# Other SBUF places for the operands of TensorE's matmuls, and one chunk temporary moved to PSUM

## The chip, the cores and the metric

The kernel runs on one core of a Trainium2 chip (trn2). The metric is the device time of one execution in microseconds; the time before is 1974.9 us, the median of 3 runs (1974.86 to 1975.0).

## What is computed

One layer of a decoder trunk on 512 tokens with 2048 features, all in float32. It has two halves:

```
x = LN(alpha*x + mixer(x))                       # pooling, convolution, two sparse attentions
gate, up = split(x @ w_gate_up)                  # 2048 -> 2 x 5632
x = LN(alpha*x + (silu(gate)*up) @ w_down)       # 5632 -> 2048
```

The mixer begins with a projection `x @ w_in` and ends with `mix @ w_out`.

## The kernel before, in words

**Precision.** Most products are split into three passes: each operand is kept as a high part (`fp32r`) and a low part (what the high part leaves), and PE computes high x high, high x low and low x high into one PSUM bank. So every block of weights is loaded by DMA, rounded to its high part by ACT (or POOL) and subtracted by DVE (or POOL) for its low part, before PE may read it. In the trace each pass has a line of its own: L795 to L797 (projection and first gate/up chunks; weights stationary, activations moving), L1030 to L1032 (output projection; activations stationary, slabs moving), L1148, L1150 and L1152 (chunks), L1197, L1199 and L1201 (down units), L1237 to L1239 (tail).

**Stages.** Until about 480 us the projection and the attention run, until 662 us the output projection, until 710 us the first two of 44 chunks of 128 hidden features. Then comes a list of 62 units (`FF_UNITS`), 42 chunk units and 20 down units, in groups of six: three chunks, two downs, one chunk. A tail forms the last four chunks' down product, adds up and normalises.

**A chunk unit** computes gate and up for 128 hidden features with a Strassen scheme: seven products instead of eight, each with 8 k-tiles x 3 passes = 24 matmuls of 256 columns. Its weight block is stationary and comes from a ring of four places in `w_room`. The moving operand is `act` in products 0, 4, 5 and 6 and one of the block sums in products 1 to 3 (`xs_1` and `xs_2` in `x_room`, `xs_4`). Between products ACT and DVE move partial results between PSUM and the temporaries `temps`. At the end h1 (tokens of the first half) and h2 (second half) are made: ACT computes silu(g2) at L1585, DVE multiplies at L2134, which sets `h2_ready`.

**A down unit** is the same scheme for the down projection, seven products of 2 x 2 x 3 = 12 matmuls of 512 columns. Here the hidden blocks are stationary (`h01`, `h23`, and their sums `hs21`, `hs4`), and the weights in the ring are moving. ACT copies d1 to d2 in PSUM after product 0 (the seed copy, L1597), for which PE waits before product 2; d2 is PSUM banks 0 and 1.

**Order.** Each engine has its instructions in a fixed order written out by hand, and semaphores join them. A ring place is written again when PE has finished the product that read it, so a block's preparation is one DMA, a possible difference of blocks (DVE), a cast (ACT, L1485) and a subtraction (DVE, L2034), up to four products ahead. POOL adds the down results to the output by DMA.

**Places.** Buffers are laid out in SBUF in the order in which the code allocates them, each at the next multiple of 32 bytes of a partition; buffers of scopes that have ended give their room back. `SHIFT` (8 elements, L102) puts the whole slabs `w_hi` and `w_lo` 32 bytes past the start of `w_room`, while the ring (`ring_hi`, `ring_lo`) ignores it; in the same way the block sums in `x_room` are shifted, and the tail's late slabs there are not. The rows of all these buffers are multiples of 512 bytes, so each buffer has one place modulo 512. Worked out from the allocations (the change's in the last column):

| buffers | read by PE in | before | with the change |
|---|---|---|---|
| ring in `w_room` | chunks, downs, tail | 192 | 192 |
| whole slabs `w_hi`, `w_lo` | projection, output projection, gate/up of the first two chunks | 224 | 256 |
| `act` | the same, and chunk products 0, 4, 5, 6 | 224 | 256 |
| block sums `xs_1`, `xs_2`, `xs_4` (and slabs that are put there for a while) | chunk products 1 to 3; some slabs of L1030 and L795 | 256 | 256 |
| `h01`, `h23`, `hs21`, `hs4` | downs, tail | 224 | 192 |
| late slabs in `x_room` | tail | 224 | 192 |
| mixing buffers, `acc`, `temps` | attention, transposes | 224 and others | all 992 bytes further; `acc`, `temps` 192 |

Of the kernel before, what the change touches and what calls it, by code (L numbers as in the profile page):

```python
# [27 lines left out]
P = 128  # L28
SEQ = 512
# [69 lines left out]


GRAN = SLAB // 2
SHIFT = 8  # L102
HALF_TOKS = SEQ // 2
S_ORDER = ("s1", "s2", "s4", "s3")
TAIL_SLOTS = ((0, 32), (2, 32), (4, 63), (5, 63), (1, 32), (3, 32), (0, 33), (2, 33))
# [36 lines left out]
def build(nc, x, x_t, w_in, w_out, pool_w, pool_scale, conv_w, conv_b, conv_ln_g, conv_ln_b, conv_pw_w,  # L142
          conv_pw_b, cmp_pos_k, cmp_pos_v, cmp_k_w1, cmp_k_w2, cmp_v_w1, cmp_v_w2, ln1_g, ln1_b,
          ln2_g, ln2_b, w_gate_up, w_down, out):
    with ExitStack() as ctx:
# [3 lines left out]
        def sem(name):  # L149
# [6 lines left out]
        w_room = sb("w_room", [P, 4 * SLAB + P + SHIFT], F32R)  # L156
        w_hi, w_lo = (w_room[:, SHIFT + at:SHIFT + at + 2 * SLAB].rearrange("p (s n) -> p s n", s=2)
                      for at in (0, 2 * SLAB + P))
        act = sb("act", [P, 2, KT, SEQ], F32R)
        act_hi, act_lo = act[:, 0, :, :], act[:, 1, :, :]  # L160
        raw = sb("raw", [P, 2, SLAB])

        mixing = ExitStack()
        with mixing:
# [35 lines left out]
        hs21 = sb("hs21", [P, 2, 2, SEQ], F32R, feed)  # L200
        stage = sb("stage", [P, 4, 2, SEQ], F32, feed)
        raw_c = sb("raw_c", [P, 2, GRAN], F32, feed)
        temps = sb("temps", [P, 5, HALF_TOKS], F32, feed)
        a12_scope = ExitStack()
        with a12_scope:
            a12 = sb("a12", [P, KT // 2, HALF_TOKS], F32, a12_scope)
# [80 lines left out]
                     "s3": act_lo[:, 0:kh, HALF_TOKS:SEQ]}  # L287
        s_source = {"s1": s1, "s2": a22, "s4": a12, "s3": a11}

        g2_temp, s_temp, p5_temp, p16_temp, p167_temp = (temps[:, i, :] for i in range(5))  # L290
        rstd_diagonal, ones_row = temps[:, 0, 0:P], temps[0:1, 0, P:2 * P]
        feed_ident, small = temps[:, 1, 0:P], temps[:, 1, P:2 * P]
        stats = small[:, 0:TT * 24].rearrange("p (i n s) -> p i n s", i=TT, n=4)
        moments = small[:, TT * 24:TT * 26].rearrange("p (i s) -> p i s", i=TT)
        rstd, shift = small[:, TT * 26:TT * 27], small[:, TT * 27:TT * 28]
        silu_g = temps[:, 3:5, :].rearrange("p a n -> p (a n)")
        r1 = [psum[:, 4 + i, 0:HALF_TOKS] for i in range(2)]
        r2, r3 = psum[:, 6, 0:HALF_TOKS], psum[:, 7, 0:HALF_TOKS]
        d1, d2, d3 = psum[:, 2:4, :], psum[:, 0:2, :], psum[:, 5:8:2, :]
# [492 lines left out]
        def _(pe):  # L792
# [457 lines left out]
            for e in range(16):  # L1250
                i, n = e // 4, e % 4
                if e < 2:
                    pe.wait_ge(x21_copied, N_DOWN)
                elif e < 4:
                    pe.wait_ge(x11_copied, N_DOWN)
                elif e >= 8:
                    pe.wait_ge(tile_added, added + e - 8 + 1)
                elif e == 4:
                    pe.wait_ge(c11_done, FF_CHUNKS - 2)
                    pe.wait_ge(g2_ready, FF_CHUNKS - 2)  # L1260
                    pe.wait_ge(c12_done, FF_CHUNKS - 1)
                for k in range(4):
                    piece = 2 * n + k // 2
                    if e == 0 and k == 0:
                        pe.wait_ge(hid_lo, hid_last - 2)
                    if k == 3 and n == 0 and i in (0, 2):
                        pe.wait_ge(hid_lo, hid_last - 1 + i // 2)
                    if i == 0 and piece < 4:
                        pe.wait_ge(lo_ready, TAIL_Q + piece + 1)
                    elif i == 0:  # L1270
                        pe.wait_ge(late_low, piece - 3)
                    w_h, w_l = late[piece - 4] if piece >= 4 else (ring_hi(TAIL_Q + piece), ring_lo(TAIL_Q + piece))
                    mm = down_products(i, k, e % 8, w_h, w_l, k % 2)
                mm.then_inc(tail_tile, 1)
# [16 lines left out]
        def _(act):  # L1291
# [232 lines left out]
            def chunk(un):  # L1524
                m, par, g = un.m, un.par, un.m // 4
                j, prev, kind = m % 2, (m - 1) % 2, m % 4
                last = g == FF_GROUPS - 1

                act.wait_ge(gran_done, un.q + 1)
                if m == 0:  # L1530
                    act.wait_ge(silu_done, 2)
                else:
                    act.wait_ge(g2_ready, m)
                nc.scalar.copy(r2, r1[par]).then_inc(p1_seeded, 1)
                unit_high(un, 4)
                if kind in (1, 2):
                    act.wait_ge(h2_ready, m)
                    part_high(h22, prev, p167_temp)
                elif m > 0:
                    act.wait_ge(h2_ready, m)  # L1540
                    part_high(h11, prev, nat[:, prev, 0:HALF_TOKS])

                act.wait_ge(gran_done, un.q + 2)
                if m > 0:
                    act.wait_ge(h1_ready, m)
                nc.scalar.copy(p5_temp, r3).then_inc(p5_copied, 1)
                unit_high(un, 5)
                if kind in (1, 2) and not last:
                    act.wait_ge(base_stored[1], 16)
                    act.wait_ge(s_nat, 6 * g + 2 * kind + 1)  # L1550
                    part_high(hs21, prev, nat[:, prev, :])
                    act.wait_ge(s_nat, 6 * g + 2 * kind + 2)
                    part_high(hs4, prev, s_temp)
                elif kind == 3 and g == FF_GROUPS - 2 or kind == 0 and last:
                    part_high(hs3, prev, nat[:, prev, HALF_TOKS:SEQ])
                elif kind in (0, 3) and m > 0:
                    act.wait_ge(s_nat, 6 * (g + (1 if kind == 3 else 0)) + prev + 1)
                    part_high(hs3, prev, s_temp)

                act.wait_ge(gran_done, un.q + 3)  # L1560
                if m == 0:
                    act.wait_ge(hid_ready, 2)
                elif kind in (1, 2):
                    act.wait_ge(hid_lo, low_count(m - 1, "a12"))
                nc.scalar.copy(p16_temp, r2).then_inc(p16_copied, 1)
                unit_high(un, 6)

                act.wait_ge(gran_done, un.q + 4)
                following(un, 0)

                act.wait_ge(gran_done, un.q + 5)
                if kind in (1, 2):
                    act.wait_ge(hid_lo, low_count(m - 1, "a22"))
                nc.scalar.copy(p167_temp, r2).then_inc(p167_copied, 1)
                following(un, 1)

                act.wait_ge(gran_done, un.q + 6)
                act.wait_ge(c22_ready, m + 1)
                nc.scalar.activation(p5_temp, r1[par], ACT.Silu).then_inc(c11_done, 1)
                following(un, 2)  # L1580

                act.wait_ge(gran_done, un.q + 7)
                if m > 0:
                    act.wait_ge(h2_ready, m)
                nc.scalar.activation(g2_temp, r2, ACT.Silu).then_inc(g2_ready, 1)  # L1585
                if kind in (0, 1):
                    act.wait_ge(h1_ready, m + 1)
                    part_high(h12, j, p16_temp)
                following(un, 3)

            def down(un):
# [2 lines left out]
                act.wait_ge(gran_done, un.q + 1)  # L1594
                if k > 0:
                    act.wait_ge(x21_copied, k)
                nc.scalar.copy(d2, d1).then_inc(down_seeded, 1)  # L1597
                unit_high(un, 4)

# [88 lines left out]
        def _(ve):  # L1688
# [388 lines left out]
            def chunk(un):  # L2077
# [53 lines left out]
                ve.wait_ge(g2_ready, m + 1)  # L2131
                ve.wait_ge(c22_ready, m + 1)
                h2 = p167_temp if kind < 2 else nat[:, j, HALF_TOKS:SEQ]
                nc.vector.tensor_tensor(h2, p167_temp, g2_temp, ALU.mult).then_inc(h2_ready, 1)  # L2134

            def down(un):
                k = un.k
# [116 lines left out]
```

## Time and profile before

| | |
|---|---|
| median of 3 runs | 1974.9 us |
| the profiled execution | 1974.57 us |
| its span in the trace | 1972.8 us |
| PE busy | 1963.5 us, 12301 matmuls |
| DVE / ACT / POOL busy | 1412.7 / 848.8 / 504.1 us |
| PE's granted clock | full (1.0) |
| DMA | 264.28 MB, 134 GB/s in the mean |

How to read it: busy time counts an engine's instructions from start to end with overlaps merged, and matmuls are pipelined, so that a matmul's duration is longer than its distance to the next. PE busy for the whole span says that it always had a matmul under way, not how densely they followed. How densely is to be had from start times in the timeline and from counts. `idle before` with an arrow tells which engine's result ended a wait.

### The profile page before, as it was taken

Reading aid. Unit: us, or ns where it says so; the run is one execution under the profiler, and the core shown is the slowest. Engines: PE = TensorE matmul, PEld = TensorE weight load, DVE = VectorE, ACT = ScalarE, POOL = GpSimd, SP = SyncE. Lnnn points to the kernel's source line nnn. Section 1 sums busy time; section 2 is a strip of 40 time slices with the busy share of each in tenths; the row PEclk is TensorE's granted clock in tenths of the full one; section 3 lists DMA queues with packets and bytes.
Section 4 is the critical chain, followed back from the end, with each engine's and each line's share of the span. In section 5 each row is a group of like instructions: output and inputs, shape, how many; then the busy total and the mean of one; then the engine's idle time right before and its main releaser. Section 6 shows DMA issues by size and latency. Waiting matters only on the chain.

```text
span 1972.8 us, 30224 instructions
## 1 busy us (share of the span) xinstructions
PE 1963.5 (100%) x12301; PEld 1732.0 (88%) x12301; DVE 1412.7 (72%) x1911; ACT 848.8 (43%) x1280; POOL 504.1 (26%) x343
## 2 busy tenths in 40 slices
PE   9999999999999999999999999999999999999999
PEld 7777888766888999998989999898998989999897
DVE  3079997263112988787878888788788878878776
ACT  3011000364000645555555555555555555555553
POOL 2555656244557310202011020201102020110200
PEclk9999999999999999999999999999999999999999
DMA  7433343500534433938466494755739376493972
GB/s 213 106 87 85 86 106 85 176 22 22 213 102 133 150 84 113 193 103 182 118 148 152 128 176 125 156 144 120 180 107 192 113 156 150 110 197 91 198 248 87
DMA packets 316429, 264.28 MB, mean 134 GB/s; under 512 B 12262, under 2 KB 258854, under 8 KB 313482
## 3 DMA queue, kind: packets, MB, share of 16 engines
q1 hardware_dynamic: 292026, 211.97, 37.4%
q0 software_dynamic: 23616, 46.15, 14.2%
q10 hardware_dynamic: 656, 4.33, 0.6%
q8 instruction: 93, 1.52, 0.3%
q14 instruction: 38, 0.31, 0.1%
HBM read 211.95 MB, written 50.33 MB: 133 GB/s over the span
## 4 chain that ended last, share of the span: by engine, by line
PE 98%; DVE 1%; DMA 1%; SPq 0%; ACT 0%; issue 0%; DVEq 0%
PE psum L1148 14%; PE psum L1150 14%; PE psum L1152 14%; PE psum L795 7%; PE psum L797 7%; PE psum L796 7%; PE psum L1199 7%; PE psum L1201 7%; PE psum L1197 7%; PE psum L1030 3%; PE psum L1031 3%; PE psum L1032 3%; PE psum L1009 1%; PE psum L946 1%; PE psum L937 1%; PE psum L997 1%
## 5 line engine op out<-in xcount | busy, mean ns | idle before, releaser
L2034 DVE TENSOR_TENSOR w_room<-raw,w_room 128x1024 fp32r<-128x1024 f32 x310 | 379.3, 1223 | 157.2 <-ACT w_room L1485 157.1
L1485 ACT CAST w_room<-raw 128x1024 fp32r<-128x1024 f32 x312 | 328.7, 1053 | 209.6 <-DVE raw L2045 67.0
L765 POOL DMA_DIRECT2D out<-stage x160 | 139.5, 1471 | 1028.4 <-DVE stage L2145 1007.6
L1148 PE MATMUL psum<-act,w_room 128*128 128x256 f32 x1344 | 375.8, 280 | 0.0
L1150 PE MATMUL psum<-act,w_room 128*128 128x256 f32 x1344 | 375.5, 279 | 0.0
L1152 PE MATMUL psum<-act,w_room 128*128 128x256 f32 x1344 | 375.3, 279 | 0.0
L1148 PEld LDWEIGHTS psum<-act,w_room 128*128 128x128 f32 x1344 | 252.7, 188 | 0.5
L1150 PEld LDWEIGHTS psum<-act,w_room 128*128 128x128 f32 x1344 | 252.6, 188 | 0.5
L1152 PEld LDWEIGHTS psum<-act,w_room 128*128 128x128 f32 x1344 | 252.8, 188 | 0.0
L795 PE MATMUL psum<-act,w_room 128*128 128x512 f32 (+2 forms) x608 | 232.0, 382 | 1.6 <-DVE act L1709 1.6
L797 PE MATMUL psum<-act,w_room 128*128 128x512 f32 (+2 forms) x608 | 229.9, 378 | 0.0
L796 PE MATMUL psum<-act,w_room 128*128 128x512 f32 (+2 forms) x608 | 229.9, 378 | 0.0
L673 POOL TENSOR_TENSOR w_room<-raw,w_room 128x2048 fp32r<-128x2048 f32 (+1 forms) x45 | 207.5, 4612 | 3.7
L2034 DVE TENSOR_TENSOR w_room<-raw_c,w_room 128x1024 fp32r<-128x1024 f32 x124 | 151.5, 1222 | 59.0 <-ACT w_room L1485 57.2
L1148 PE MATMUL psum<-x_room,w_room 128*128 128x256 f32 x672 | 185.6, 276 | 0.0
L1152 PE MATMUL psum<-x_room,w_room 128*128 128x256 f32 x672 | 185.5, 276 | 0.0
L1150 PE MATMUL psum<-x_room,w_room 128*128 128x256 f32 x672 | 185.5, 276 | 0.0
L670 POOL TENSOR_SCALAR w_room<-raw 128x2048 fp32r<-128x2048 f32 (+1 forms) x45 | 88.8, 1973 | 259.7 <-PE psum L797 136.6
L795 PEld LDWEIGHTS psum<-act,w_room 128*128 128x128 f32 (+1 forms) x608 | 113.8, 187 | 27.3 <-issue 5.1
L797 PEld LDWEIGHTS psum<-act,w_room 128*128 128x128 f32 (+1 forms) x608 | 113.8, 187 | 22.1
L796 PEld LDWEIGHTS psum<-act,w_room 128*128 128x128 f32 (+1 forms) x608 | 113.8, 187 | 22.0 <-issue 0.5
L1485 ACT CAST w_room<-raw_c 128x1024 fp32r<-128x1024 f32 x126 | 132.7, 1053 | 0.0
(303 smaller groups left out, 4131.9 us busy)
## 6 DMA issues: line engine op xcount, KB each, us to landing
raw_c<-in_w_gate_up SPq DMA_DIRECT2D x84, 512.0 KB, 6.6
raw<-in_w_gate_up SPq DMA_DIRECT2D x84, 512.0 KB, 5.6
out<-stage POOLq DMA_DIRECT2D x160, 256.0 KB, 8.2
raw<-in_w_in SPq DMA_DIRECT2D x30, 1024.0 KB, 5.8
raw<-in_w_down SPq DMA_DIRECT2D x46, 512.0 KB, 4.7
raw_c<-in_w_down SPq DMA_DIRECT2D x42, 512.0 KB, 3.8
raw<-in_w_out SPq DMA_DIRECT2D x16, 1024.0 KB, 5.1
acc<-in_x SPq DMA_DIRECT2D x1, 4096.0 KB, 12.4
```

The costliest lines, as they stand in the source:

```text
L673: nc.gpsimd.tensor_tensor(lo, raw[:, slot, 0:words], hi.bitcast(F32), ALU.subtract)\
L765: nc.gpsimd.dma_start(out_dram[:, tile, n * SEQ:(n + 1) * SEQ], part, accum_op=ALU.add)\
L795: nc.tensor.matmul(out_ap, stat_hi, mov_hi, start=first, stop=False)
L796: nc.tensor.matmul(out_ap, stat_hi, mov_lo, start=False, stop=False)
L797: return nc.tensor.matmul(out_ap, stat_lo, mov_hi, start=False, stop=last)
L1148: nc.tensor.matmul(out_ap, stat_hi[:, cols], mov_hi[:, k, :], start=opens and k == 0, stop=False, skip_group_check=not opens)
L1150: nc.tensor.matmul(out_ap, stat_hi[:, cols], mov_lo[:, k, :], start=False, stop=False, skip_group_check=not opens)
L1152: mm = nc.tensor.matmul(out_ap, stat_lo[:, cols], mov_hi[:, k, :], start=False, stop=k == kh - 1, skip_group_check=not opens)
L1197: nc.tensor.matmul(out_ap[:, i, :], room[:, 0, j, toks], w_h[:, cols], start=opens and j == 0, stop=False, skip_group_check=not opens)
L1199: nc.tensor.matmul(out_ap[:, i, :], room[:, 1, j, toks], w_h[:, cols], start=False, stop=False, skip_group_check=not opens)
L1485: nc.scalar.copy(ring_hi(at), src).then_inc(hi_ready, 1)
L2034: nc.vector.tensor_tensor(lo, src, hi.bitcast(F32), ALU.subtract).then_inc(lo_ready, 1)
```

## The change

`SHIFT` becomes 16 elements (64 bytes). Two buffers that nothing reads or writes are put in: `below_act` (512 bytes) ahead of `act`, and `between` (448 bytes) after `raw`. `temps` loses one of its five slices of 1024 bytes: the result of silu for the second token half, `g2_temp`, now lies in PSUM, in the right half (columns 256 to 511) of bank 1, for the last chunk unit of bank 6 (`g2_room`). The other temporaries move up by one slice and keep their roles. 64 bytes for the two shifts, 512 and 448 more and 1024 less leave the block sums at their old address (179968). Bank 1 is also part of d2, so ACT waits for h2 of the chunk before ahead of the seed copy of every even down unit, and PE waits for the last h2 before output tile 4 of the tail.

```diff
-SHIFT = 8
+SHIFT = 16
...
+        below_act = sb("below_act", [P, P])
         act = sb("act", [P, 2, KT, SEQ], F32R)
         act_hi, act_lo = act[:, 0, :, :], act[:, 1, :, :]
         raw = sb("raw", [P, 2, SLAB])
+
+        between = sb("between", [P, P - SHIFT])
...
-        temps = sb("temps", [P, 5, HALF_TOKS], F32, feed)
+        temps = sb("temps", [P, 4, HALF_TOKS], F32, feed)
...
-        g2_temp, s_temp, p5_temp, p16_temp, p167_temp = (temps[:, i, :] for i in range(5))
-        rstd_diagonal, ones_row = temps[:, 0, 0:P], temps[0:1, 0, P:2 * P]
-        feed_ident, small = temps[:, 1, 0:P], temps[:, 1, P:2 * P]
+        s_temp, p5_temp, p16_temp, p167_temp = (temps[:, i, :] for i in range(4))
+        g2_room = [psum[:, bank, HALF_TOKS:SEQ] for bank in (1, 6)]
+        rstd_diagonal, ones_row = temps[:, 1, 0:P], temps[0:1, 1, P:2 * P]
+        feed_ident, small = temps[:, 0, 0:P], temps[:, 0, P:2 * P]
...
-        silu_g = temps[:, 3:5, :].rearrange("p a n -> p (a n)")
+        silu_g = temps[:, 2:4, :].rearrange("p a n -> p (a n)")
...
                     pe.wait_ge(c12_done, FF_CHUNKS - 1)
+                    pe.wait_ge(h2_ready, FF_CHUNKS - 2)
...
-                nc.scalar.activation(g2_temp, r2, ACT.Silu).then_inc(g2_ready, 1)
+                nc.scalar.activation(g2_room[m == FF_CHUNKS - 3], r2, ACT.Silu).then_inc(g2_ready, 1)
...
                     act.wait_ge(x21_copied, k)
+                if k % 2 == 0:
+                    act.wait_ge(h2_ready, 4 * (k // 2) + 3)
                 nc.scalar.copy(d2, d1).then_inc(down_seeded, 1)
...
-                nc.vector.tensor_tensor(h2, p167_temp, g2_temp, ALU.mult).then_inc(h2_ready, 1)
+                nc.vector.tensor_tensor(h2, p167_temp, g2_room[m == FF_CHUNKS - 3], ALU.mult).then_inc(h2_ready, 1)
```

## Rows read from the trace of the kernel before

**Rows 1.** The page: span, busy time of each engine, the chain that ended last.
```profile
span 1972.8 us, 30224 instructions
...
PE 1963.5 (100%) x12301; PEld 1732.0 (88%) x12301; DVE 1412.7 (72%) x1911; ACT 848.8 (43%) x1280; POOL 504.1 (26%) x343
...
PE 98%; DVE 1%; DMA 1%; SPq 0%; ACT 0%; issue 0%; DVEq 0%
```

**Rows 2.** PE's waits: us in total, times, longest.
```profile
PE psum L795 <- DVE act L1709: 1.6, 2, 1.3
```

**Rows 3.** PE's groups by form: line, shapes, count | busy us, mean ns.
```profile
L1148 PE MATMUL psum<-act,w_room 128*128 128x256 f32 x1344 | 375.8, 280 | 0.0
...
L1148 PE MATMUL psum<-x_room,w_room 128*128 128x256 f32 x672 | 185.6, 276 | 0.0
...
L1197 PE MATMUL psum<-w_room,h 128*128 128x512 f32 x320 | 126.5, 395 | 0.0
...
L1197 PE MATMUL psum<-w_room,hs 128*128 128x512 f32 x240 | 94.9, 396 | 0.0
...
L795 PE MATMUL psum<-act,w_room 128*128 128x512 f32 x528 | 207.4, 393 | 1.6 <-DVE act L1709 1.6
...
L1030 PE MATMUL psum<-w_room,act 128*128 128x512 f32 x224 | 87.7, 392 | 0.0
...
L1237 PE MATMUL psum<-w_room,h 128*128 128x512 f32 x32 | 12.7, 396 | 0.0
```

**Rows 4.** PE's timeline, units 14 to 16: start us, duration us, line, operands.
```profile
983.43 0.28 PE L1148 MATMUL psum<-act,w_room 128*128 128x256 f32 x1
...
986.23 0.28 PE L1148 MATMUL psum<-x_room,w_room 128*128 128x256 f32 x1
...
994.39 0.28 PE L1148 MATMUL psum<-act,w_room 128*128 128x256 f32 x1
...
1002.80 0.39 PE L1197 MATMUL psum<-w_room,h 128*128 128x512 f32 x1
...
1042.00 0.28 PE L1148 MATMUL psum<-act,w_room 128*128 128x256 f32 x1
```

**Rows 5.** PE's matmuls of one line in a window: count, duration min/median/max ns, first and last start.
```profile
L795 PE MATMUL psum<-act,w_room x208: 389/389/389, 196.2 to 336.9; 128*128 128x512 f32 x104
...
L1030 PE MATMUL psum<-x_room,act x8: 393/396/399, 624.7 to 629.6; 128*128 128x512 f32 x8
...
L795 PE MATMUL psum<-act,w_room x16: 283/283/283, 682.4 to 687.8; 128*128 128x256 f32 x16
...
L795 PE MATMUL psum<-act,xs x16: 395/396/397, 688.1 to 698.6; 128*128 128x512 f32 x16
```

**Rows 6.** Timelines of DVE, ACT and PE's weight loads around the first down unit.
```profile
995.67 1.23 DVE L2034 TENSOR_TENSOR w_room<-raw,w_room 128x1024 fp32r<-128x1024 f32 x1 [0.28 <-ACT w_room L1485]
...
1006.31 0.42 DVE L2134 TENSOR_TENSOR nat<-temps 128x256 f32<-128x256 f32 x1
...
994.59 1.05 ACT L1485 CAST w_room<-raw 128x1024 fp32r<-128x1024 f32 x1 [1.40 <-PE psum L1152]
...
1005.80 1.00 ACT L1597 COPY psum<-psum 128x1024 f32<-128x1024 f32 x1 [1.47 <-PE psum L1201]
...
1008.17 0.19 PEld L1197 LDWEIGHTS psum<-w_room,hs 128*128 128x128 f32 x1
```

**Rows 7.** ACT's and DVE's groups by form, operands in SBUF and in PSUM.
```profile
L1585 ACT ACTIVATE temps<-psum 128x256 f32<-128x256 f32 x42 | 16.2, 385 | 17.1 <-PE psum L1152 17.1
...
L1534 ACT COPY psum<-psum 128x256 f32<-128x256 f32 x42 | 15.0, 357 | 42.1 <-PE psum L1152 42.1
...
L1546 ACT COPY temps<-psum 128x256 f32<-128x256 f32 x42 | 15.7, 373 | 34.8 <-PE psum L1152 34.8
...
L2110 DVE TENSOR_TENSOR temps<-psum,temps 128x256 f32<-128x256 f32 x42 | 17.5, 416 | 0.3 <-PE psum L1152 0.2
```

**Rows 8.** One chunk unit (14): busy us of each engine (count), PEclk, DMA share, GB/s.
```profile
983.43:1002.80 19.37, 19.37 (x170) 19.37 (x169) 17.32 (x24) 10.76 (x17) 0.00 (x0) 1.00 0.34 110
```
## The prediction

> **What bounds the kernel now.** I read the page first: TensorE (PE) is busy for 1963.5 of 1972.8 us, and the chain that ended last is 98% PE [rows 1]. Its waits come next: the longest of them adds up to 1.6 us [rows 2]. So nobody feeds PE too late, and time can only go by way of PE's matmuls: fewer, or closer together. Their number stays at 12301 here, so the question is the spacing.
>
> A matmul's duration is no spacing, for matmuls overlap: L1148 shows 280 ns on `act` and 276 ns on `x_room` [rows 3], but the timeline has about 116 ns from one start to the next. I take spacings from start times and known counts. Of chunk unit 14, product 0 (24 matmuls, moving operand in `act`) runs from 983.43 to 986.23: 2.80 us / 24 = 116.7 ns. Products 1 to 3 (72 matmuls, moving operand in the block sums) end at 994.39: 8.16 / 72 = 113.3 ns. Products 4 to 6 (72, `act` again) end at 1002.80: 8.41 / 72 = 116.8 ns [rows 4]. Same shape, same engine, same ring of weights; what differs is the moving operand's place. With the table of places above, in bytes modulo 512:
> - 256 columns, ring at 192: moving at 256 (64 past it) 113.3 ns; moving at 224 (32 past it) 116.8 ns.
> - 256 columns, both at 224: 16 matmuls of L795 start within 5.4 us, with two others after each, so 5.4 / 45 = 120.0 ns [rows 5].
> - 512 columns, both at 224: 140.7 us / (207 x 3) = 226.6 ns [rows 5].
> - 512 columns, places 32 apart: the two down units, 168 matmuls from 1002.80 to 1042.00, 233.3 ns [rows 4]; moving 256 and stationary 224 (L1030 on `x_room`) 4.9 / 21 = 233.3 ns; moving 224 and stationary 256 (L795 on `xs`) 10.5 / 45 = 233.3 ns [rows 5].
> The spacing thus goes with the difference of the two places, whichever operand lies higher, and in opposite order for the two lengths: at 512 columns equal places are cheap, at 256 columns they are dear and 64 apart is cheap. The clock is not in it: granted clock 1.00 in this unit [rows 8].
>
> **The change part by part, on PE.**
> 1. *Activations from 32 to 64 past the ring.* Four of seven products of each of the 42 chunk units: 1344 x 3 lines = 4032 matmuls [rows 3], from 116.8 to 113.3 ns. 4032 x 3.48 ns = 14.0 us. The block sums keep their address and so their 113.3.
> 2. *h blocks from 32 past the ring to the ring's place.* (320 + 240) x 3 = 1680 matmuls of the 20 down units [rows 3] from 233.3 to 226.6 ns: 1680 x 6.7 = 11.3 us. The tail's products on the ring, 32 x 3 = 96 [rows 3], 0.6 us. Its products on the late slabs stay at equal places (both move from 224 to 192): nothing.
> 3. *Whole slabs at the activations' new place.* Slabs and activations move together, so all that ran at 226.6 (or 120.0) stays there. What gains are the products whose slab lay in the block-sum rooms at 256, now equal: 96 on `x_room` and 48 on `xs`, 144 x 6.7 = 1.0 us (16 of L795 and 8 per token tile of L1030 [rows 5], three passes, four tiles).
> Sum on PE: 14.0 + 11.3 + 0.6 + 1.0 = 26.9 us.
> 4. *The mixing stage's buffers* move by one common 992 bytes; the 32-bit products there have both operands among them. Nothing, and 0.5 us either way for loads that land at other addresses at the start.
>
> **The parts off PE.**
> 5. *silu(g) of the second half goes to PSUM instead of SBUF.* ACT's Silu takes 385 ns; a copy out of PSUM takes 373 ns into SBUF and 357 ns into PSUM [rows 7], so at most 16 ns less. The multiply that reads it takes 0.42 us [rows 6], and the add with one operand in PSUM 416 ns [rows 7]. Nothing.
> 6. *A new wait of ACT ahead of the seed copy* (L1597) of every even down unit, ten in all: it now waits for h2 of the chunk before, since both use PSUM bank 1. Behind it on ACT stand the seed copy, for which PE waits before product 2, and the cast of a weight block, which VectorE (DVE) waits for. Before, the seed started at 1005.80, and h2 was made from 1006.31 to 1006.73 [rows 6]. So the seed moves to about 1006.77 and ends at 1007.77. PE's first weight load of product 2 started at 1008.17 [rows 6], 0.40 us later. But PE gets faster: h2 hangs on a row of DVE work that starts with the cast at 994.59 [rows 6], after product 3, so between there and the load three `act` products (72 x 3.48 ns = 0.25 us) and two down products (24 x 6.7 = 0.16 us) go by 0.41 us sooner. The cover of 0.40 us is just used up. I charge 0.1 us a time, 1.0 us in all; bounds: nothing, and 0.4 us a time, 4 us. The cast is late by under 1 us, and its products start 5 us later: nothing.
> 7. *The tail's extra wait of PE on h2* is met before output tile 4, after 48 matmuls, some 11 us into the tail; h2 lands 3.9 us after its unit's end (1006.73 against 1002.80 [rows 4, 6]). Nothing.
> 8. *DVE, DMA.* In a chunk unit DVE is busy for 17.32 of 19.37 us [rows 8]; the unit shrinks by 96 x 3.48 = 0.33 us. DVE stays covered, by 1.7 us. DMA engines are busy for a third of it.
>
> Sum: 26.9 - 1.0 = 25.9 us. The profiled execution took 1974.57 us, the median is 1974.9, 0.3 above it: 1974.9 - 25.9 = 1949.0.
>
> **Where the Trainium skill speaks against this.** In the rows, the distance between two operands moves the spacing by 3 to 7 ns [rows 4, 5]. The Trainium skill, "TensorE: Matmul & The Clock Gate", section "Step-by-step: what each phase is for", says that weight loads and the moving operand have read ports of their own, so that loading the next weights takes nothing from the running matmul. By that rule places would not matter and the sum would be 0. The same page, "Back-to-back issue gap", has N / 2.4 + 2.5, an estimate of 109.2 and 215.8 ns; the trace has 113.3 at best and 226.6, so here something is left even at the good places.
>
> **The rivals.**
> - *Places do nothing* (0.03): the differences come from strides or from which matmul follows, 1974.9, or 1976 with the new wait. Against it: three different pairs of buffers 32 apart all give 233.3 ns.
> - *One of the two moves fails* (0.07). `act` has 2048 bytes from one k to the next, the sums 1024; if that is why they differ, 14.0 us are lost: 1963. If h at 192 stays at 233.3, 11.3 are lost: 1960.
> - *The wait costs more* (0.06): 0.4 to 1 us each time it is met, on ten units 4 to 10 us: 1952 to 1958. It is met if DVE's row reaches h2 later than I follow it.
> - *Places on multiples of 64 are good in themselves* (0.05): all 224 places vanish, and equal pairs at 192 or 256 could drop to twice 113.3. Some 4300 matmuls of 512 columns by 6.5 ns give another 28 us: 1921. For it: 224 is in every dear pair. Against: 120.0 and 226.6 come from one and the same pair of places.
> - *Slower: the slabs' stage pays* (0.03). No matmul of 512 columns has been seen with both operands at 256. If what was good was 224 itself, 2256 matmuls (528 x 3 of L795's group, 224 x 3 of L1030's [rows 3]) go from 226.6 to 233.3: +15.1 us; if then the other places don't behave either, nothing comes back: 1990. With no gain elsewhere it decides from 1.7 ns a matmul, with the full gain only from 13 ns.
>
> **How the numbers follow.** The forecast has 0.76. Its own range: the spacings from two-digit starts are good to 0.2 ns, some 1.5 us together; the wait gives 1 us less or 3 more; with the start's 0.5 this is 1946 to 1953. To hold 8 in 10 it takes in the nearer part of the dear wait and a little below: 1945 to 1955. About 0.2% (3.9 us) is what a measurement of this kernel can tell from no change. Faster by more than that: forecast, half, wait and the 64-rival, 0.94. Within: nothing from places, 0.03. Slower: 0.03.
>
> **What would show it.** In the profile after: L1148 on `act` at 276 ns instead of 280, L1197 at 389 instead of 396, with starts 113.3 and 226.6 apart; L795 and L1030 on `w_room` unchanged at 389; L1030 on `x_room` at 389. A chunk unit of 19.04 us, a down unit of 19.04 us. The seed copy starting right after h2, about 1 us later against the down unit's start, and waits of PE for the seed copy of at most a few us in ten pieces. Wrong if `act` stays at 280 (stride), if L795 goes to 396 (224 was good in itself), or if PE's waits show ten gaps of over 0.4 us.

## The result, and the profile after

| | before | after |
|---|---|---|
| median of the runs | 1975.0 us (13 runs, 1974.07 to 1976.75) | 1978.43 us (13 runs, 1977.58 to 1981.4) |
| the profiled execution | 1974.57 us | 1980.94 us |
| its span | 1972.8 us | 1979.1 us |

The ratio of after to before is 1.0020, 95% interval 1.0011 to 1.0028. The forecast was 1949.0, the range 1945 to 1955: it is missed by 29 us, and the sign is wrong. What a measurement can tell from no change was put at 0.2%; the change sits on that bound, on the slow side.

The page of after, span and busy time (as [rows 1]):

```profile
span 1979.1 us, 30226 instructions
...
PE 1968.9 (99%) x12301; PEld 1748.6 (88%) x12301; DVE 1412.5 (71%) x1911; ACT 845.8 (43%) x1280; POOL 503.8 (25%) x343
```

PE's waits of after, the one with the largest total (as [rows 2]; us in total, times, longest):

```profile
PE psum L799 <- DVE act L1716: 2.1, 2, 1.2
```

The list has no wait of PE in the downs and none for the seed copy. Whatever was lost was lost in the spacing, as the prediction's first part said it would have to be. PE's groups by form in after (columns as in [rows 3]; L1148 has become L1152, L1197 L1201, L795 L799, L1030 L1034, L1237 L1241):

```profile
L1152 PE MATMUL psum<-act,w_room 128*128 128x256 f32 x1344 | 376.2, 280 | 0.0
...
L1152 PE MATMUL psum<-x_room,w_room 128*128 128x256 f32 x672 | 188.1, 280 | 0.0
...
L1201 PE MATMUL psum<-w_room,h 128*128 128x512 f32 x320 | 124.7, 390 | 0.0
...
L1201 PE MATMUL psum<-w_room,hs 128*128 128x512 f32 x240 | 93.4, 389 | 0.0
...
L1034 PE MATMUL psum<-x_room,act 128*128 128x512 f32 x32 | 12.6, 392 | 0.0
...
L1241 PE MATMUL psum<-w_room,h 128*128 128x512 f32 x32 | 12.5, 390 | 0.0
```

The downs (L1201) fell from 395 and 396 ns to 390 and 389, as forecast. The chunks did not: `act` stays at 280, and the group on `x_room`, the block sums, which the change leaves exactly where they were, beside a ring that it leaves too, rose from 276 to 280. Nothing in the prediction had those move. The start times of the same chunk unit (timeline of after, as [rows 4]):

```profile
985.71 0.28 PE L1152 MATMUL psum<-act,w_room 128*128 128x256 f32 x1
...
988.53 0.28 PE L1152 MATMUL psum<-x_room,w_room 128*128 128x256 f32 x1
...
997.01 0.28 PE L1152 MATMUL psum<-act,w_room 128*128 128x256 f32 x1
...
1005.49 0.40 PE L1201 MATMUL psum<-w_room,h 128*128 128x512 f32 x1
...
1043.61 0.28 PE L1152 MATMUL psum<-act,w_room 128*128 128x256 f32 x1
```

Product 0 takes 2.82 us / 24 = 117.5 ns (117.8 within the rounding of the starts), products 1 to 3 8.48 / 72 = 117.8, products 4 to 6 8.48 / 72 = 117.8. The unit has 19.78 us instead of 19.37. The two downs take 38.12 us / 168 = 226.9 ns, against 39.20 before.

**Where the time went.** The span is 6.3 us longer. The 62 units begin at 711.61 (710.67 before) and end with the tail's first matmul at 1923.8 (1917.0 before), so 0.9 us comes ahead of them, 5.9 us in them, and the tail gives back 0.6. In the units 42 x 0.41 us = 17 us is lost in chunks (0.6 us less, since the first unit of before, with 19.92 us, and the second, with 19.45, were slow already) and 10 x 1.08 = 11 us won in downs. Ahead of them the whole slabs' 1.0 us was won, and about 1.9 us lost to something else: a stretch at about 408 us that ran at the half clock.

Busy time by stretches of after (columns: window; its length and busy us of PE, PEld, DVE, ACT, POOL with counts; granted clock; DMA share; GB/s):

```profile
406.00:408.00 2.00, 2.00 (x18) 1.90 (x18) 0.17 (x1) 0.00 (x0) 0.00 (x0) 1.00 0.00 0
408.00:412.00 4.00, 4.00 (x7) 1.56 (x6) 2.07 (x4) 0.00 (x0) 0.00 (x0) 0.57 0.00 0
412.00:414.00 2.00, 2.00 (x6) 0.93 (x5) 0.24 (x1) 0.79 (x2) 0.00 (x0) 1.00 0.00 0
```

In these rows PE is busy all the time before, during and behind the stretch. Its clock was at the upper level (2.4 GHz), fell for part of these 4 us to the lower one (1.2 GHz), and came back. The 32 matmuls of that line (L941) take 653 ns in the mean here and 595 in the kernel before, which makes the 1.9 us. The profiled execution of after is 2.5 us above the median of its runs; corrected for this stretch it is 1979.0. The places are not what brings it: e2 below, with all places as before, shows a granted clock of 0.57 from 476 to 480 us, e6 and e10 show 0.57 and 0.62 from 406 to 410, and e3, e4, e7, e8, e9 and e11 show no such stretch.

### The profile page after: what moved, and what is told of

Its sections match the earlier page's. It is cut to its first block, busy times and chain, and to the rows that moved or that the text cites. A ratio compares the mean times of both kernels' runs of the same rounds, so it can differ in the third digit from the quotient of the medians.

```text
span 1979.1 us, 30226 instructions
## 1 busy us (share of the span) xinstructions
PE 1968.9 (99%) x12301; PEld 1748.6 (88%) x12301; DVE 1412.5 (71%) x1911; ACT 845.8 (43%) x1280; POOL 503.8 (25%) x343
## 4 chain that ended last, share of the span: by engine, by line
PE 98%; DVE 1%; DMA 0%; ACT 0%; issue 0%; SPq 0%; DVEq 0%
PE psum L1152 14%; PE psum L1156 14%; PE psum L1154 14%; PE psum L799 7%; PE psum L801 7%; PE psum L800 7%; PE psum L1201 6%; PE psum L1203 6%; PE psum L1205 6%; PE psum L1034 3%; PE psum L1036 3%; PE psum L1035 3%; PE psum L1013 1%; PE psum L950 1%; PE psum L941 1%; PE psum L1001 1%
## 5 line engine op out<-in xcount | busy, mean ns | idle before, releaser
L1152 PE MATMUL psum<-act,w_room 128*128 128x256 f32 x1344 | 376.2, 280 | 0.0
L1152 PEld LDWEIGHTS psum<-act,w_room 128*128 128x128 f32 x1344 | 252.2, 188 | 0.4
L799 PE MATMUL psum<-act,w_room 128*128 128x512 f32 (+2 forms) x608 | 231.8, 381 | 2.4 <-DVE act L1716 2.1
L1152 PE MATMUL psum<-x_room,w_room 128*128 128x256 f32 x672 | 188.1, 280 | 0.0
L1156 PE MATMUL psum<-x_room,w_room 128*128 128x256 f32 x672 | 187.5, 279 | 0.0
L1154 PE MATMUL psum<-x_room,w_room 128*128 128x256 f32 x672 | 187.5, 279 | 0.0
L674 POOL TENSOR_SCALAR w_room<-raw 128x2048 fp32r<-128x2048 f32 (+1 forms) x45 | 89.0, 1979 | 259.2 <-PE psum L801 136.5
L799 PEld LDWEIGHTS psum<-act,w_room 128*128 128x128 f32 (+1 forms) x608 | 113.8, 187 | 27.6 <-issue 4.9
```

Source lines behind the costliest of these rows:

```text
L799: nc.tensor.matmul(out_ap, stat_hi, mov_hi, start=first, stop=False)
L1152: nc.tensor.matmul(out_ap, stat_hi[:, cols], mov_hi[:, k, :], start=opens and k == 0, stop=False, skip_group_check=not opens)
L1154: nc.tensor.matmul(out_ap, stat_hi[:, cols], mov_lo[:, k, :], start=False, stop=False, skip_group_check=not opens)
L1156: mm = nc.tensor.matmul(out_ap, stat_lo[:, cols], mov_hi[:, k, :], start=False, stop=k == kh - 1, skip_group_check=not opens)
```

## The experiments

**Theory after the result.** "Distance" is from here on how many bytes, within a partition, the operand that comes from activations (in chunk units the moving one, in down units the h block, which is stationary) lies past the one in the ring of weights; the tests of 256 and of 512 columns copy these two cases. PE's pace at one pair of places may have two steady values, and what ran ahead decides which. In the kernel before, 24 matmuls at distance 32 come ahead of products 1 to 3; after the change nothing at distance 32 is left. A rival: h blocks, activations or the PSUM move disturb the chunks in some other way (stride, bank, wait). One place of the old trace, which the prediction had not looked at, speaks for the theory: the very first chunk unit of the kernel before (its timeline, first matmul of product 1 and of product 4):

```profile
713.47 0.28 PE L1148 MATMUL psum<-x_room,w_room 128*128 128x256 f32 x1
...
721.95 0.28 PE L1148 MATMUL psum<-act,w_room 128*128 128x256 f32 x1
```

8.48 / 72 = 117.8 ns, with the same operands at the same places that gave 113.3 in unit 14 [rows 4].

**e1: a map of distances, matmuls alone.** Blocks of 24 matmuls of 256 columns (three passes over eight k-tiles, a ring of four) or 12 of 512 columns; the stationary or the moving operand is shifted. The rest of the computation is left out.

```diff
+            for op in (o for _ in range(1) for o in block_512(0)): nc.tensor.matmul(*op, start=True, stop=True)
+            for op in first(24, (o for _ in range(3) for o in block_256(32))): nc.tensor.matmul(*op, start=True, stop=True)
+            for op in (o for _ in range(3) for o in block_256(64)): nc.tensor.matmul(*op, start=True, stop=True)
```

> Only matmuls, in the shapes and order of chunk units (256 columns, passes hi-hi, hi-lo, lo-hi, ring of four blocks) and of down units (512 columns), on a buffer that nothing else uses: the rest of the computation is left out. Tests of 72 matmuls of 256 columns at each distance of 0, 32, ... 480 bytes between moving operand and ring, entered from 512 columns at distance 0, from 256 columns at distance 32, and from 512 columns at distance 32; then 12 tests of distance 64 entered after 24 to 35 matmuls at distance 32. Theory 1 (PE's pace at one distance has two steady values, and what ran before chooses): at distance 64 some entries give 113.3 ns and others 117.8 ns from start to start, and the twelve entries of different length don't all give the same; at distance 32 116.7 or 120.0. Theory 2 (the slow pace of the block-sum products comes from other engines' traffic or from PSUM): with no other engine at work distance 64 is 113.3 ns whatever came before. At 512 columns both expect 226.7 at distance 0 and 233.3 at 32.

It took 1097.97 us. Single lines of its trace (duration in ns min/median/max, first and last start in us). The last runs of it are the triples of the diff: 12 matmuls of 512 columns at equal places, n of 256 at distance 32, 72 at distance 64. The rows are the last part, for n = 24, 25, 26, 27:

```profile
L193 PE MATMUL psum<-room x72: 275/276/277, 859.3 to 867.3; 128*128 128x256 f32 x72
...
L196 PE MATMUL psum<-room x72: 279/279/284, 873.1 to 881.5; 128*128 128x256 f32 x72
...
L199 PE MATMUL psum<-room x72: 275/276/277, 887.4 to 895.4; 128*128 128x256 f32 x72
...
L202 PE MATMUL psum<-room x72: 279/279/284, 901.4 to 909.8; 128*128 128x256 f32 x72
```

Even n gives 8.0 us / 71 = 113 ns, odd n 8.4 / 71 = 118 ns, for all twelve n from 24 to 35. From the start times to the nanosecond the two values are 113.3 and 117.8. No other engine is at work here, so the slow pace needs neither traffic nor results in PSUM from others: theory 2 is out. The map itself: what counts of a distance is its remainder modulo 256 bytes (0 to 224 and 256 to 480 give the same values), not modulo 512 as the table of places had it. Entered from 512 columns at equal places, 256 columns go at 120.0 ns at distance 0, 116.7 at 32, 117.8 at 64, 120.0 at 96 and 128; 512 columns at 226.7 at distance 0 and 229 to 234 at the other multiples of 32. The way in matters at distance 32 too: behind 72 matmuls at distance 0 it held 117.8 over 168 matmuls, where the expectation had 116.7 or 120.0, and the 72 at distance 64 behind them (L115) went at 117.8 although 168 is even. So distance 64 is no good place in itself, and 32 is not worse than it: entered in that way, it is better.

**e2, e3, e4: one part of the change at a time.** e2 has the PSUM temporary and the waits alone, all places as before. e3 and e4 move one group of operands each:

```diff
 # e3: h blocks at the ring's place, activations and slabs still 32 past it
 SHIFT = 16
+SLABS = 8
-        below_act = sb("below_act", [P, P])
+        below_act = sb("below_act", [P, P - 8])
...
 # e4: activations and slabs 64 past the ring, h blocks still 32 past it
-SHIFT = 16
+SHIFT = 8
+SLABS = 16
```

> Only silu's result in PSUM and its waits; all places as before. Theory 1: chunk products stay at 116.8 (activations) and 113.3 ns (block sums), time within 1.5 us of before, the rest being the new wait. Theory 2 (PSUM or the new traffic slows PE): block sums near 117.8 ns, which is 42 x 72 x 4.4 ns = 13 us more than before.

> h blocks at the ring's place as in the change, activations and whole slabs back at 32 past it. Both theories expect down units at 226.7 ns (11 us less, tail 0.6 less). Theory 1: activations' products at 116.7 or 120.0 and block sums at 113.3 or 117.8, by how the handover from 32 to 64 falls: 1963 us if it falls as before, up to 1982 if not. Theory 2: block sums at 117.8 with activations at 116.8, near 1976.

> Activations and whole slabs at 64 past the ring as in the change, h blocks back at 32 past it. Down units 233.3 ns. Theory 1: all seven products of a chunk unit at one pace, 117.8 ns if entering from 512 columns at distance 32 leads to the slow value (1990 us), 113.3 if to the fast one (1960 us). Theory 2: activations 113.3 or 117.8, block sums 117.8.

e2: 1975.89 us, ratio 0.9999 (0.9990 to 1.0009). The PSUM part and the waits cost nothing, and spacings stay as before. e3: 1963.34 us, ratio 0.9938 (0.9921 to 0.9954): the h blocks' 11 us, whole. e4: 1989.95 us, ratio 1.0072 (1.0056 to 1.0089): the whole loss. Timeline of e3, chunk unit 14 from product 1, and the ends of its two downs:

```profile
983.37 0.28 PE L1153 MATMUL psum<-x_room,w_room 128*128 128x256 f32 x1
...
991.53 0.28 PE L1153 MATMUL psum<-act,w_room 128*128 128x256 f32 x1
...
999.94 0.40 PE L1202 MATMUL psum<-w_room,h 128*128 128x512 f32 x1
...
1038.04 0.28 PE L1153 MATMUL psum<-act,w_room 128*128 128x256 f32 x1
```

Block sums 8.16 / 72 = 113.3 ns, `act` at distance 32 8.41 / 72 = 116.8, downs 38.10 / 168 = 226.8. The same of e4:

```profile
984.99 0.28 PE L1153 MATMUL psum<-act,w_room 128*128 128x256 f32 x1
...
1004.78 0.39 PE L1202 MATMUL psum<-w_room,h 128*128 128x512 f32 x1
...
1043.97 0.28 PE L1153 MATMUL psum<-act,w_room 128*128 128x256 f32 x1
```

The chunk unit takes 19.79 us / 168 = 117.8 ns, the downs 39.19 / 168 = 233.3. So `act` at distance 64 spoils the chunks, block sums included, whether the downs before are at distance 0 or 32.

**e5: more ways in, steps of 16 bytes.** Matmuls alone again; the rest of the computation is left out.

> Only matmuls again, the computation is left out. After 12 matmuls of 512 columns at distance 0 come 1 to 8 of 256 columns at distance 32 and then 72 at distance 64. By the first map, where 24, 26, ... 34 at distance 32 led to 113.3 ns and 25, 27, ... 35 to 117.8, theory 1 expects the same split by even and odd here, perhaps the other way round for the shortest, whose first starts are uneven. Two at distance 32 and then 504 at 64: the pace of the start holds to the end. Further tests give the steady pace for every 16 bytes of distance; a rival to theory 1, that the slow pace creeps in with time, expects 504 matmuls to end slower than they begin.

It took 974.33 us. Source lines of its trace; ahead of each 12 matmuls of 512 columns at equal places, then n of 256 columns at distance 32, then those of the row at distance 64: n = 1 (L80), 2 (L83), 7 (L98), 8 (L101), 2 with 504 behind them (L104), none with 504 (L106). L122 is 72 matmuls at distance 112, entered directly.

```profile
L80 PE MATMUL psum<-room x72: 278/279/281, 42.7 to 51.0; 128*128 128x256 f32 x72
...
L83 PE MATMUL psum<-room x72: 275/276/277, 54.1 to 62.2; 128*128 128x256 f32 x72
...
L98 PE MATMUL psum<-room x72: 278/279/284, 112.2 to 120.6; 128*128 128x256 f32 x72
...
L101 PE MATMUL psum<-room x72: 275/276/277, 124.4 to 132.5; 128*128 128x256 f32 x72
...
L104 PE MATMUL psum<-room x504: 275/276/277, 135.6 to 192.6; 128*128 128x256 f32 x168
...
L106 PE MATMUL psum<-room x504: 278/279/283, 195.4 to 254.7; 128*128 128x256 f32 x168
...
L122 PE MATMUL psum<-room x72: 274/275/282, 336.6 to 344.7; 128*128 128x256 f32 x72
```

Two matmuls at another distance are enough, one is not, and both values last: 57.0 us / 503 = 113.3 ns, 59.3 / 503 = 117.9 ns (117.8 from the start times to the nanosecond). Neither pace drifts into the other. Distance 112 falls into the fast one from this way in, after a first third at 115 ns.

The same run holds a limit of the count. Behind 36 matmuls of 512 columns at a distance that changes from test to test come 24 of 256 columns at distance 32 and then 24 at distance 64. The last 24, where the 512 columns stood at distance 32 (L181) and at 48 (L184):

```profile
L181 PE MATMUL psum<-room x24: 279/279/281, 700.5 to 703.2; 128*128 128x256 f32 x24
...
L184 PE MATMUL psum<-room x24: 276/276/279, 714.5 to 717.1; 128*128 128x256 f32 x24
```

The same 24, an even number, lead to the fast pace behind 512 columns at 0, 16, 48, 96, 160, 176, 192 and 224, and to the slow one behind 32, 64, 80, 112, 128, 144 and 208. So even and odd decide only with the matmuls ahead of them held fixed. And behind downs at distance 32, as the kernel before has them, this test gives the slow pace where that kernel ran fast: the count alone does not foretell it.

**e6, e7, e8: matmuls put ahead, in the changed kernel.** Ahead of product 0 of the eleven chunk units that open a run of chunks, whose result product 0 then overwrites:

```diff
+KICKS = 2
...
+                if m % 4 == 3 or first:
+                    pe.wait_ge(lo_ready, un.q + 1)
+                    for _ in range(KICKS):
+                        nc.tensor.matmul(r1[par], ring_hi(un.q)[:, 0:P], act_hi[:, kh, 56:56 + HALF_TOKS],
+                                         start=True, stop=True)
                 product(un, 0, r1[par], act_hi[:, 0:kh, early], act_lo[:, 0:kh, early], True)
```

Element 56 is 224 bytes, so the moving operand is 288 past the ring, 32 modulo 256. e7 has one of them; e8 has two that begin at element 0, at distance 64.

> The changed kernel with two more matmuls (256 columns, distance 32 modulo 256, result overwritten) before product 0 of each chunk unit that follows a down unit, and of the first one. Theory 1: if two is a number that leads to the fast pace, chunk units run at 113.3 ns: 7056 x 4.45 ns = 31.4 us less than the changed kernel, 22 x 0.12 = 2.6 us of matmuls more, so 1949 to 1950; if it is not, 117.8 ns and 1981. Theory 3 (there is no memory, the slow pace belongs to the changed kernel's places): 1981.

> The same with one more matmul instead of two. Theory 1: the other pace than with two, so 1979.5 if two leads to the fast pace, 1948 if two leads to the slow one. Theory 3: 1979.5.

> The same two extra matmuls at distance 64, the distance of those that follow. Theory 1: they change nothing in the pace, 117.8 ns throughout and 1981 us. A rival (any extra work or the extra wait at a chunk unit's start resets the pace) expects the same time as with two at distance 32.

e6: 1950.21 us, ratio 0.9875 (0.9858 to 0.9891). e7: 1981.0, ratio 1.0030 (1.0018 to 1.0041). e8: 1982.24, ratio 1.0038 (1.0022 to 1.0053). Timeline of e6, the same chunk unit, its downs and the two added matmuls (L1171):

```profile
977.82 0.28 PE L1153 MATMUL psum<-act,w_room 128*128 128x256 f32 x1
...
980.54 0.28 PE L1153 MATMUL psum<-x_room,w_room 128*128 128x256 f32 x1
...
988.70 0.28 PE L1153 MATMUL psum<-act,w_room 128*128 128x256 f32 x1
...
996.86 0.39 PE L1207 MATMUL psum<-w_room,h 128*128 128x512 f32 x1
...
1034.96 0.40 PE L1171 MATMUL psum<-act,w_room 128*128 128x256 f32 x2
1035.20 0.28 PE L1153 MATMUL psum<-act,w_room 128*128 128x256 f32 x1
```

19.04 us / 168 = 113.3 ns in all products, and this is the 19.04 us that the prediction gave for a chunk unit. Groups by form, on `act` in e6 and then in e7 and e8:

```profile
L1153 PE MATMUL psum<-act,w_room 128*128 128x256 f32 x1344 | 371.0, 276 | 0.0
```

```profile
L1155 PE MATMUL psum<-act,w_room 128*128 128x256 f32 x1344 | 376.4, 280 | 0.0
```

```profile
L1155 PE MATMUL psum<-act,w_room 128*128 128x256 f32 x1344 | 376.3, 280 | 0.0
```

The wait and the number of matmuls are the same in e6 and e8; only the 224 bytes differ. e6 and e7 differ by one matmul. e6 is 28 us below the changed kernel and faster than both.

**e9: another common distance, nothing put ahead.** Ring and h blocks stay; activations, slabs and block sums go to 112 bytes past the ring.

```diff
-SHIFT = 16
+SHIFT = 28
...
-        act = sb("act", [P, 2, KT, SEQ], F32R)
+        act_room = sb("act_room", [P, 4 + 2 * KT * SEQ], F32R)
+        act = act_room[:, 4:4 + 2 * KT * SEQ].rearrange("p (a k n) -> p a k n", a=2, k=KT)
...
+            xs_4_room = sb("xs_4_room", [P, 60 + 2 * SLAB], F32R, s4_scope)
```

> The changed kernel with another common place: activations, whole slabs, block sums and the slabs put into their rooms all lie 112 bytes past the ring's place modulo 256; the ring, the h blocks and the late slabs stay at 192 modulo 256. No matmul is added. In the two runs of matmuls alone, 256 columns at distance 112 went at 113.3 ns from both ways in that were tried, at most a few ns slower in their first third. Theory (a distance of 64 has two steady paces, one of 112 only the fast one): all 7056 matmuls of the chunk units go at 113.3 ns instead of 117.8, 7056 x 4.45 ns = 31.4 us below the changed kernel's 1978.4: 1947 us, the two downs stay at 226.7, L795 and L1030 too, since slabs and activations stay equal. Rival (the fast pace belongs to what runs ahead, not to the distance): 117.8 again, 1978. Rival (what was good was a multiple of 64 in the addresses): slower than 1978.

It took 1960.87 us, ratio 0.9933 (0.9916 to 0.9949): 14 us above the theory's 1947. Groups by form of e9:

```profile
L1152 PE MATMUL psum<-act_room,w_room 128*128 128x256 f32 x1344 | 369.7, 275 | 0.0
...
L1152 PE MATMUL psum<-x_room,w_room 128*128 128x256 f32 x672 | 184.8, 275 | 0.0
...
L799 PE MATMUL psum<-act_room,w_room 128*128 128x512 f32 x528 | 209.6, 397 | 1.7 <-DVE act_room L1716 1.6
...
L1034 PE MATMUL psum<-w_room,act_room 128*128 128x512 f32 x224 | 89.1, 398 | 0.0
```

And L799 from 170 to 310 us, of after and then of e9:

```profile
L799 PE MATMUL psum<-act,w_room x207: 389/389/389, 169.7 to 309.8; 128*128 128x512 f32 x104
```

```profile
L799 PE MATMUL psum<-act_room,w_room x202: 394/394/394, 170.2 to 309.5; 128*128 128x512 f32 x101
```

The chunks did what was expected of them: all at 113.3 ns (the first product behind the downs 115), with nothing put ahead of them. But the 512-column stage, for which 226.7 was taken because slabs and activations stay equal, went to 139.3 us / (201 x 3) = 231.0 ns, against 140.1 / (206 x 3) = 226.7. Some 1632 matmuls x 4.3 = 7 us. In the output projection L1034's 672 matmuls have 7 ns more in their durations, and their start times lie 233.2 ns apart instead of 226.9, another 4 to 5 us: 11 to 12 of the 14 us. Both operands at 48 modulo 256 is not as good as both at 224, 192 or 0: equal places are not enough, the place itself counts too.

**e10, e11: the rule turned against a good kernel.** e3, with one and with two matmuls at distance 32 put at the same eleven places.

```diff
 # on e3
+KICKS = 1   # e11: 2
...
+                        nc.tensor.matmul(r1[par], ring_hi(un.q)[:, 0:P], act_hi[:, kh, 0:HALF_TOKS],
+                                         start=True, stop=True)
```

> The kernel with the h blocks moved alone (activations still 32 past the ring), and ONE matmul of 256 columns at distance 32 added ahead of product 0 of the eleven chunk units that open a run of chunks. Theory (an odd number of matmuls at distance 32 ahead of those at 64 leads into the slow pace): those units but the first of all fall to the values of unit 0 of the kernel before (about 117.8 in products 1 to 3, 120 in products 5 and 6), 10 x 0.54 us, the next unit's product 0 is at 120, 10 x 0.08 us, the very first unit may turn fast (0.5 us less), and the added ones cost 11 x 0.12 = 1.3 us: 1963.3 + 6.9 = 1970 us. Rival (matmuls ahead only ever help, or do nothing but take their own time): 1964.6 us, products 1 to 3 at 113.4 everywhere.

> The same with TWO matmuls added at each of the eleven places. Theory (parity): nothing changes but their own time, 22 x 0.117 = 2.6 us: 1966 us, products 1 to 3 at 113.4 in all units but the very first. Rival (any matmul that is added there disturbs): as slow as with one, 1970 us or above.

e10: 1977.94 us, ratio 1.0013 (1.0004 to 1.0023). e11: 1965.82, ratio 0.9956 (0.9939 to 0.9972), where 1966 was expected. One matmul more costs 14.6 us over e3, two cost 2.5. Timeline of e10, unit 14 from product 1 to the first down:

```profile
988.14 0.28 PE L1154 MATMUL psum<-x_room,w_room 128*128 128x256 f32 x1
...
996.62 0.28 PE L1154 MATMUL psum<-act,w_room 128*128 128x256 f32 x1
...
1005.02 0.40 PE L1208 MATMUL psum<-w_room,h 128*128 128x512 f32 x1
```

Block sums at 8.48 / 72 = 117.8 ns, `act` at 8.40 / 72 = 116.7. The direction was right and the size was not (1970 was expected): unit 14 is the last of its run of four, and it is as slow as the first. The expectation had copied what the very first units of the kernel before do (one slow, the next fast). By the rule itself the 96 matmuls at distance 32 between one unit's block sums and the next unit's are an even number and change nothing, so the whole run stays slow: by the start times of all units 41 of the 42, 40 of them fast in e3, 40 x 72 x 4.5 ns = 13 us, with 1.3 us for the added ones 14 us. That fits. The first run of units does not follow the count. Its first unit is slow with none added (before) and with one, fast with two (e11), where the wait ahead of the added ones differs as well. And its pace changes on its own behind that: in the kernel before from the first unit to the second, in e10 from the second to the third, each time over 96 matmuls at distance 32, most of which went at 120.0 ns instead of 116.7.

## Why the prediction was wrong

**Step 1 failed** (activations from 32 to 64 past the ring, 14.0 us won; "The block sums keep their address and so their 113.3"). It took the spacing as a function of the two places alone: "moving at 256 (64 past it) 113.3 ns; moving at 224 (32 past it) 116.8 ns". Both numbers are right, but 113.3 is one of two steady paces of that pair, and which one comes hangs on the matmuls that the step moved away: 24 at distance 32 ahead of the block sums. With the downs at equal places, 24, 25 and 26 of them give 113.3, 117.8 and 113.3 (e3, e10, e11). With the downs at distance 32 the kernel before was fast with 24 in all ten runs of units that follow downs; e5's short copy of that order was slow, so for this way in the count is no explanation, and what makes it fast stays open. With all seven products at 64 and the downs ahead of them the pair has 117.8. That cost 4.4 ns on the 3024 matmuls on the block sums (13.4 us, nowhere in the sum) and 1.0 ns on the 4032 on `act` (4.2 us, forecast as 14.0 won), less some 0.6 for the slow first units of before: 17 us lost where 14 were to be won. e4 shows the loss by itself, e6 undoes it with 22 matmuls.

**Step 2 was right.** Downs 226.9 ns instead of 233.3, 11 us in e3 and in the changed kernel; the tail's 0.6 us too.

**Step 3 was right** for what it named: L1034 on `x_room` has 389 ns in its median, and L799 and L1034 on `w_room` stayed. Two of the spacings it rests on were read from starts with one digit (4.9 / 21 is good to some 5 ns, 10.5 / 45 to 2), too coarse to tell 226.6 from 233.3; the start times to the nanosecond give 233.4 and 233.2 before and 227 after, so it was right with some luck. It held for a move to 256; e9 shows that a common move is not free at every place.

**Steps 4 and 5 were right.** Step 4: the output projection begins at 478.80 us before and at 480.52 after, 478.6 without the half-clock stretch; it moved by 0.2 us, within the 0.5 that were allowed, and no run moves these buffers alone. Step 5: e2 is the kernel before within 0.1%.

**Step 6 was right in its times, and its charge did not come.** Timelines of ACT, DVE and weight loads of after around the first down unit, as [rows 6]:

```profile
1009.45 1.00 ACT L1604 COPY psum<-psum 128x1024 f32<-128x1024 f32 x1 [2.44 <-DVE nat L2141]
```

```profile
1008.93 0.41 DVE L2141 TENSOR_TENSOR nat<-temps,psum 128x256 f32<-128x256 f32 x1
```

```profile
1010.75 0.19 PEld L1201 LDWEIGHTS psum<-w_room,hs 128*128 128x128 f32 x1
```

The seed copy waits for h2, starts 3.96 us into the down (forecast 3.97) and ends 0.30 us before the weight load of product 2. PE's list of waits has no line for it: 0, not 1.0 us. But this is not the case that the step reckoned with, for the chunks had not become faster. e6 is: there the down starts at 996.86, the seed copy ends at 1002.14, and PE's first weight load of product 2 starts at 1002.18, 0.04 us later. The cover is just used up, as the step said, and still no wait is listed. Step 7 cost nothing either; step 8 was not tried at the full speed of the chunks until e6, which kept DVE at 17.22 of 19.04 us without a wait of PE.

With step 1 replaced by what was measured of it, and the wait at nothing, the sum is 1974.9 + 17 - 11.3 - 0.6 - 1.0 = 1979, and 1978.4 was measured.

**The rivals.** None was this one. "One of the two moves fails" was nearest, and its signature came true (`act` at 280); but its reason, the stride of `act`, falls with e6, where the same strides run at 276, and its price counted only what was hoped for, not what the block sums had to lose. The slower rival looked to the 512-column stage and had the wrong place. The Trainium skill, "TensorE: Matmul & The Clock Gate", section "Step-by-step: what each phase is for", by which a weight load takes nothing from the running matmul, was weighed there and set aside, rightly so far as places go: e1 has the same instructions at 113.3 to 120.0 ns by places and by what ran ahead. No run here leaves the weight loads out, so whether it is they that take the time is not shown. The same page of the Trainium skill, "Back-to-back issue gap", has a formula for a matmul by itself that gives an estimate of 109.2 ns for 256 columns; the best of any run here is 113.3.

**What could have been seen before.** The first chunk unit of the old trace has 117.8 ns at the places that are called good. Spacings had been taken from one unit; a look at all 42 for the same pair of places would have shown two values, and with them that the step's price had a branch of the other sign: 7056 matmuls at 117.8 are 17 us more than the mixture of before.

## What to carry to other kernels

Before a spacing is put down to places, take it from every stretch that has them, the first included: a pair of places that shows two values has a state, and the state belongs to what runs ahead. When a step moves all operands onto the "good" distance, ask which matmuls at the other distance it takes away, and what those did for their neighbours. Where a steady loop sits in the slower pace, two cheap matmuls at another distance ahead of it, or a distance that falls into the fast pace by itself, are worth a try: here they took 28 us off, their own 2.6 us included. The number that works has to be tried again after every change of what stands ahead: behind other matmuls the same 24 led to the other pace (e5).

## What the runs showed of the hardware

- **Two steady paces.** 256 columns, moving operand 64 bytes past the stationary one modulo 256: 113.3 or 117.8 ns from start to start, each held over 504 matmuls. Behind 512-column matmuls at equal places (e1, e5), each even number tried (2 to 8, 24 to 34) of matmuls at distance 32 leads to the fast one, none and each odd number tried (1 to 7, 25 to 35) to the slow one. Behind 512 columns at other distances 24 lead to the fast pace in some cases and to the slow one in others (e5).
- **Distance 32 has more than one pace too**: 116.7 ns in most runs, 117.8 in e1 behind 72 matmuls at distance 0, 120.0 in the first unit of the kernel before.
- **The period is 256 bytes**, in the distance of the two operands: in e1, 120.0, 116.7 and 117.8 ns at 0, 32 and 64 come again at 256, 288 and 320. Of the sixteen distances in steps of 16 bytes (e5, entered from 512 columns at equal places) only 112 settles at 113.3 ns; 512 columns go at 226.7 at 0, 16, 144 and 240.
- **Equal places at 512 columns** give 226.7 ns at 192, 224 and 256; at 304 (48 modulo 256) they give 231.0 in the projection and 233.2 in the output projection (e9).
- **Half clock.** In the profiled execution of after PE's granted clock was 0.57 in the mean of 408 to 412 us, with PE busy for all of it; it cost 1.9 us. The profiled kernel before shows 1.00 there. Three of the nine other full kernels profiled have such a stretch, among them e2 with the places of before; what brings it is open.
- Open is also what in PE makes the two paces: the runs show the rule of even and odd, not its cause, and neither the first run of chunk units nor the way in from downs at distance 32 follows it.
